# Eight accumulating units multiply in plain fp32 from the loaded weights instead of from a high/low split

## The chip, the cores and the metric

The kernel runs on one core of one Trainium2 chip. The metric is device time in microseconds (us) of one execution; the number shown for a kernel is the median of its runs. Engine names are those of the profile: PE (TensorE), PEld (its weight loads), DVE (VectorE), ACT (ScalarE), POOL (GpSimd), SP (SyncE, here the issuer of most DMAs).

## The reference, cut to what matters

The reference is a three-layer network on 256 tokens of width 2048. The change sits in the first 200 us, in the start of the first layer:

```
mod    = silu(c) @ w_ada + b_ada             # 6 x 2048 values; shift1, scale1 are the first two
h      = rms_norm(x, g) * (1 + scale1) + shift1
proj   = h @ w_in                            # lru_x, lru_gate, q, k, v, g_a, g_b
xc     = causal_depthwise_conv(lru_x)        # then the recurrence, attention, feed-forward, ...
```

Activations are kept transposed (features on the 128 partitions, 256 tokens along the free axis), so a tensor of width 2048 is 16 blocks of 128x256. The first two pieces of `mod` are needed before any block of h exists: block b needs 128 columns of shift1 and of scale1.

## The kernel before, in words

**Units and chunks.** Every matrix product is cut into units of 256 output columns, and a unit into chunks of 512 input rows: a chunk is one DMA of 512 KB, a tile of 128x1024 fp32. Products are made with fp32 split in two parts of a narrower format (fp32r): ACT copies the raw tile to `whi` (L976), DVE subtracts to get `wlo` (L1361), and h is split likewise into Hhi and Hlo. A product is then hi*hi + hi*lo + lo*hi. There are four slots (NSP) for split tiles; ACT and DVE split up to three chunks ahead of PE.

**The first stage, in four quarters.** The eight units `lrux` produce lru_x. They are not done one after the other: quarter q of the input rows (4 blocks of h) is multiplied for all eight units, each unit holding its own PSUM bank through all four quarters (part = open, more, more, close). For each chunk, `products` (L672 to L709) issues 24 matmuls of 128x128 by 128x256: 4 blocks, 2 output halves, 3 products (L690, L691, L692). Only after the last quarter are the banks read out (ACT L1197, DVE L1822). Then come the eight q units, which use `products_wide` (L725, L733).

**Where h comes from.** 16 vector-matrix rows of w_ada per quarter are reduced on DVE: each is a half row block of 128x1024, multiplied with silu(c) (tile CR) and summed in one instruction (L1402, followed by a read of the accumulator). When the sixteenth of a quarter is done, `first_columns` (L1373 to L1382) adds halves and bias and makes A1v, the scale. ACT `norm1` (L987) then computes, per block, Hhi (L991) and a full-precision copy in TG (L995), and DVE subtracts to get Hlo (L1442). The normalised x (XR) comes from DVE L1436, two instructions per quarter. The rms itself needs x to be loaded, eight squares on ACT (L1315), sixteen fp32 products with ones on PE (L910, L911), then DVE L1416, L1421, a root on ACT and a Newton step (L1425 to L1431).

**The stream of loads.** SP issues one DMA after the other from an ordered list, `stream` (L656): first 12 rows for `ada`, then two weight chunks, then 4 more ada, then six times (weight, ada, ada). From there each quarter repeats: two weights, 4 ada, six times (weight, ada, ada); the last quarter has weights only in its second part. Two weights, 4 ada and six triples are 24 loads. In this stage the tiles go round nine raw buffers, so load n must wait until load n-9 is no longer needed, and everything behind it in the list waits too:

```
for el in stream:
    if el.prev >= 0:
        sp.wait_ge(s_freed[done[el.prev][0]], done[el.prev][1])
    sp.dma_start(raw[el.slot][:, 0:el.n], source(el)).then_inc(s_raw[el.slot], 16)
```

A buffer is free when DVE has made wlo from it (`s_lo`) or has reduced it (`s_ada`). Ahead of the list SP issues `vec` (small vectors) and the two halves of c (L649); ACT's queue loads constants (L1304) and x (L1305, 2 MB); POOL's queue loads two small tables. DVE takes its work in the order of the list too (`feed`).

**What else hangs on the stage.** POOL loads four tiles of gate weights (L2046) once all 16 blocks of Hlo exist; PE needs them for the gates (L746), plain fp32 matmuls after the q unit 1 has begun.

Of the kernel before, what the change touches and what calls it, by code (L numbers as in the profile page):

```python
# [89 lines left out]
def _plan():  # L90
# [114 lines left out]
    def weight(un, c):  # L205
        un.chunks.append(len(order))
        order.append(len(stream))
        stream.append(Elem("w", 4 * un.width, (un.src, un.u, un.kc0 + un.corder[c]), ord=len(order) - 1))

    coming = quarter(0)  # L210
    rest = [(b, h) for b in range(32, 96) for h in range(2)]
# [33 lines left out]
    for i, el in enumerate(stream):  # L245
        allowed = [n for k, n in rings if k <= i][-1]
        r = next(r for r in ring if r in allowed)
        ring.remove(r)
        ring.append(r)
        used[r] += 1  # L250
        el.slot, el.landed, el.prev, el.first = r, 16 * used[r], owner.get(r, -1), r not in owner
        owner[r] = i

        key = "ada" if el.kind == "ada" else "split"
        counts[key] += 1
        done.append((key, counts[key]))
# [125 lines left out]
def _build(nc, ctx, d_x, d_mem, d_c, d_vec, d_cst, d_hot, d_relb, d_ada, d_lru, d_w, d_s2, d_out):  # L382
# [110 lines left out]
    s_hi, s_lo, s_mm = sem("hi"), sem("lo"), sem("mm")  # L493

    s_ct, s_cr, s_ada, s_mod = (sem(n) for n in ("ct", "cr", "ada", "mod"))
    s_freed = {"split": s_lo, "ada": s_ada}

    kinds = list(dict.fromkeys(u.kind for u in units))
    s_ev = {k: sem(f"ev_{k}") for k in kinds}
# [7 lines left out]
    s_mup, s_mu, s_sh, s_zc, s_zs, s_totz, s_td, s_cen, s_cenp = (  # L507
        sem(n) for n in ("mup", "mu", "sh", "zc", "zs", "totz", "td", "cen", "cenp"))

    s_xr, s_sl, s_slp, s_hh, s_h, s_hp = (sem(n) for n in ("xr", "sl", "slp", "hh", "h", "hp"))  # L510

    s_sp, s_gt, s_gsb, s_gms, s_pre, s_lg, s_lt, s_ls, s_lm, s_lu, s_la, s_sr, s_scan = (
        sem(n) for n in ("sp", "gt", "gsb", "gms", "pre", "lg", "lt", "ls", "lm", "lu", "la", "sr", "scan"))
# [30 lines left out]
    split_no, mem_no = {}, {}  # L544
    n_split = 0
    for i, el in enumerate(stream):
        if el.kind != "ada":
            n_split += 1
            split_no[i] = n_split
            if el.kind == "mem":  # L550
                mem_no[el.g, el.kt] = n_split
# [93 lines left out]

    def sync(sp):
        sp.dma_start(vec[:, :], d_vec).then_inc(s_vec, 16)
        for h in range(2):
            sp.dma_start(CR[h][:, :], d_c[:, h * CH:(h + 1) * CH]).then_inc(s_c, 16)  # L649
        for el in stream:  # L650
            if el.prev >= 0:
                sp.wait_ge(s_freed[done[el.prev][0]], done[el.prev][1])
            elif el.slot == 5:

                sp.wait_ge(s_lg, 16)
            sp.dma_start(raw[el.slot][:, 0:el.n], source(el)).then_inc(s_raw[el.slot], 16)  # L656
        for b in range(1, NB, 2):
            sp.wait_ge(s_hh, 64 + b + 1)
            sp.dma_start(d_out[:, b - 1:b + 1, :], RES[:, b - 1:b + 1, :]).then_inc(s_out, 16)
        sp.wait_ge(s_out, 8 * 16)  # L660


    def tensor(pe):
# [8 lines left out]
        def products(un, c):  # L672

            ch = un.chunks[c]
            s, w = ch % NSP, un.width
            pe.wait_ge(s_lo, split_no[order[ch]])
            xh, xl, _ = tensors[un.x]
            ps = banks[un.bank]
            start = c == 0 and un.part in ("", "open")
            stop = c == un.nkc - 1 and un.part in ("", "close")  # L680
            for k in range(4):
                kt = 4 * un.corder[c] + k
                if begins[un.x] is un or un.part and un.j == 0:
                    pe.wait_ge(*ready[un.x](kt))
                end = stop and k == 3
                if un.mode == "f":
                    for i in range(2):
                        o, at_ = ps[:, i * 256:(i + 1) * 256], k * w + i * 128
                        h, lo = whi[:, s, at_:at_ + 128], wlo[:, s, at_:at_ + 128]
                        pe.matmul(o, h, xh[:, kt, :], start=start, stop=False, skip_group_check=True)  # L690
                        pe.matmul(o, h, xl[:, kt, :], start=False, stop=False, skip_group_check=True)  # L691
                        ins = pe.matmul(o, lo, xh[:, kt, :], start=False, stop=end and i == 1, skip_group_check=True)  # L692
                        start = False
                elif un.mode == "t":
                    h, lo = whi[:, s, k * w:(k + 1) * w], wlo[:, s, k * w:(k + 1) * w]
                    for t in range(2):
                        o, tk = ps[:, t * 256:(t + 1) * 256], slice(t * 128, (t + 1) * 128)
                        pe.matmul(o, xh[:, kt, tk], h, start=start, stop=False, skip_group_check=True)  # L698
                        pe.matmul(o, xh[:, kt, tk], lo, start=False, stop=False, skip_group_check=True)  # L699
                        ins = pe.matmul(o, xl[:, kt, tk], h, start=False, stop=end and t == 1, skip_group_check=True)  # L700
                        start = False
                else:
                    h, lo = whi[:, s, k * w:(k + 1) * w], wlo[:, s, k * w:(k + 1) * w]
                    o = ps[0:w, 0:256]
                    pe.matmul(o, h, xh[:, kt, :], start=start, stop=False, skip_group_check=True)
                    pe.matmul(o, h, xl[:, kt, :], start=False, stop=False, skip_group_check=True)
                    ins = pe.matmul(o, lo, xh[:, kt, :], start=False, stop=end, skip_group_check=True)
                    start = False
            ins.then_inc(s_mm, 1)  # L709

        def products_wide(un, c):


            ch = un.chunks[c]
            s = ch % NSP
            xh, _, both = tensors[un.x]
            out = [banks[un.bank + i] for i in range(2)]
            pe.wait_ge(s_hi, split_no[order[ch]])
            for k in range(4):
                kt = 4 * un.corder[c] + k  # L720
                if begins[un.x] is un:
                    pe.wait_ge(*ready[un.x](kt))
                for i in range(2):
                    at_ = k * 256 + i * 128
                    pe.matmul(out[i].rearrange("p (a s) -> p a s", a=2), whi[:, s, at_:at_ + 128], both[:, :, kt, :],  # L725
                              start=(c == 0 and k == 0), stop=False, skip_group_check=True)
            pe.wait_ge(s_lo, split_no[order[ch]])
            high = slice(256, 512) if un.x in ("Y0", "Y1") else slice(0, 256)
            for k in range(4):
                kt = 4 * un.corder[c] + k  # L730
                for i in range(2):
                    at_ = k * 256 + i * 128
                    ins = pe.matmul(out[i][:, high], wlo[:, s, at_:at_ + 128], xh[:, kt, :], start=False,  # L733
                                    stop=(c == un.nkc - 1 and k == 3), skip_group_check=True)
            ins.then_inc(s_mm, 1)
# [178 lines left out]
        for st in steps:  # L914
# [22 lines left out]
            elif un.part == "open" and un.bank == 4:  # L937
                clear("S")
            for c in range(un.nkc):
                if un.wide < 0:  # L940
                    products(un, c)
                else:
                    products_wide(un, c)
# [19 lines left out]
    def scalar(act):  # L963
# [21 lines left out]
                                   ACT.Copy).then_inc(s_hi, 1)  # L985

        def norm1(q):  # L987
            act.wait_ge(s_mod, q + 1)
            for b in range(4 * q, 4 * q + 4):
                act.wait_ge(s_xr, b // 2 + 1)  # L990
                act.activation(Hhi[:, b, :], XR[:, b, :], ACT.Identity, scale=A1v[:, b:b + 1],  # L991
                               bias=mod[:, b:b + 1]).then_inc(s_hh, 1)
                if b >= 4:
                    act.wait_ge(s_h, b - 3)
                act.activation(tslot(b), XR[:, b, :], ACT.Identity, scale=A1v[:, b:b + 1],  # L995
                               bias=mod[:, b:b + 1]).then_inc(s_slp, 1)

        def gates(j, n):
            yield from ticks(n)
# [298 lines left out]
        def centre_first(l):  # L1298
# [2 lines left out]
            yield  # L1301
            centred(l, 1)

        act.dma_start(cst[:, 0:C_DUP], d_cst[:, 0:C_DUP]).then_inc(s_cst, 16)  # L1304
        act.dma_start(RES[:, :, :], d_x).then_inc(s_x, 16)  # L1305
        act.wait_ge(s_c, 32)
        for h in range(2):
            act.activation(CT[:, h, :], CR[h][:, :], ACT.Tanh, scale=0.5).then_inc(s_ct, 1)
        act.wait_ge(s_lx, 1)
        act.activation(LPS[:, 3, :], LPS[:, 2, :], ACT.Exp, scale=-1.0).then_inc(s_le, 1)  # L1310
        act.wait_ge(s_x, 16)
        for j in range(8):
            if j >= 2:
# [39 lines left out]
    def vector(dve):  # L1353
# [39 lines left out]
        def feed(upto):  # L1393
            nonlocal pos
            while pos <= upto:
                el, i = stream[pos], pos
                pos += 1
                if el.kind != "ada":
                    low(i, el)
                    continue  # L1400
# [35 lines left out]
                dve.tensor_tensor(XR[:, 2 * j:2 * j + 2, :], RES[:, 2 * j:2 * j + 2, :], over(Rv, 2), ALU.mult).then_inc(s_xr, 1)  # L1436

        def norm1(q):
            for b in range(4 * q, 4 * q + 4):
                dve.wait_ge(s_hh, b + 1)  # L1440
                dve.wait_ge(s_slp, b + 1)
                dve.tensor_tensor(Hlo[:, b, :], tslot(b), v32(Hhi[:, b, :]), ALU.subtract).then_inc(s_h, 1)  # L1442
            if q < 3:
                scaled(q + 1)

        def log1p_exp(e, d, s, q, p, k):

# [449 lines left out]
        for st in steps:  # L1897
# [31 lines left out]
            if un.part in ("open", "more"):  # L1929
                continue  # L1930
            evac(un)
            side.tick()
        side.flush()

# [241 lines left out]
```

## Time and profile before

| what | value |
|---|---|
| median of 3 runs | 2794.49 us (2793.2 to 2797.61) |
| the profiled execution's own time | 2798.37 us |
| its span | 2796.2 us |
| PE busy | 2675.8 us, 96% of the span |
| DVE busy | 1995.4 us, 71% |
| ACT busy | 1449.3 us, 52% |
| DMA, bytes read | 574 MB, 206 GB/s over the span |

Busy time of PE counts from the start of a matmul to a modelled end and overlaps are merged, so a share near 100% need not be PE at its peak: the distance between two starts is the better measure of a matmul. The granted clock of TensorE (PEclk) is 1.00 at 2.4 GHz and 0.50 at 1.2 GHz. Times in the timeline are counted from the start of the span.

### The profile page before, as it was taken

To read this page: it belongs to the slowest core of one execution; us is meant where nothing else is said; L and a number is where in the kernel's file an instruction comes from. 1 tells how busy PE (TensorE), PEld (TensorE's weight loads), DVE (VectorE), ACT (ScalarE), POOL (GpSimd) and SP (SyncE) were. 2 spreads that over 40 slices of the span, in tenths; PEclk is the share of its full clock that TensorE was granted. 3 is DMA by queue.
4 is the path that set the end of the run, shared out by engine and by line. 5 is a ranking of instruction groups with operands and counts; after the bars stand their busy time and mean duration, and the time that the engine had idled before them with its cause. 6 is when DMAs were issued, how large, how long until landed. Compare 5 with 4: busy or idle time off the path is not lost.

```text
span 2796.2 us, 40818 instructions
## 1 busy us (share of the span) xinstructions
PE 2675.8 (96%) x16090; PEld 2360.1 (84%) x16090; DVE 1995.4 (71%) x2806; ACT 1449.3 (52%) x2167; POOL 141.1 (5%) x177
## 2 busy tenths in 40 slices
PE   4789799999999999999999999999999999999996
PEld 4778688888888788888888888888988888889885
DVE  7987888887899866666666676666566766664666
ACT  3355566655545554455545545544554455445543
POOL 0000000000001000000000010100001121000002
PEclk8899899999999999999999999999999999999998
DMA  8964577788889776656566655665546556665452
GB/s 330 375 215 151 173 254 244 264 261 274 289 300 330 260 253 191 194 188 189 183 194 188 189 186 158 190 181 174 155 147 195 182 179 176 182 181 158 143 177 103
DMA packets 162109, 584.10 MB, mean 209 GB/s; under 512 B 19040, under 2 KB 20320, under 8 KB 161792
## 3 DMA queue, kind: packets, MB, share of 16 engines
q1 hardware_dynamic: 157104, 566.86, 62.6%
q0 software_dynamic: 4528, 12.43, 1.6%
q8 instruction: 127, 2.08, 0.3%
q10 hardware_dynamic: 288, 2.23, 0.2%
q14 instruction: 62, 0.51, 0.1%
HBM read 574.05 MB, written 2.15 MB: 206 GB/s over the span
## 4 chain that ended last, share of the span: by engine, by line
PE 83%; DVE 12%; ACT 3%; issue 1%; DMA 0%; ACTq 0%; SPq 0%; DVEq 0%
PE bank L725 47%; PE bank L733 24%; DVE wlo L1361 3%; DVE raw L1402 3%; PE bank L698 2%; PE bank L700 2%; PE bank L699 2%; PE pO L782 1%; PE pS L759 1%; ACT whi L976 1%; PE pT L771 1%; DVE TG L1489 1%; DVE XC L1822 1%; PE pS L812 1%; DVE bank L1808 1%
## 5 line engine op out<-in xcount | busy, mean ns | idle before, releaser
L1361 DVE TENSOR_TENSOR wlo<-raw,whi 128x1024 fp32r<-128x1024 f32 (+1 forms) x880 | 1075.7, 1234 | 447.5 <-ACT whi L976 443.7
L976 ACT ACTIVATE whi<-raw 128x1024 fp32r<-128x1024 f32 (+1 forms) x880 | 911.5, 1048 | 437.1 <-PE bank L733 342.6
L725 PE MATMUL bank<-H,whi 128*128 128x512 f32 x4000 | 1021.1, 397 | 4.5 <-DVE H L1673 3.6
L725 PEld LDWEIGHTS bank<-H,whi 128*128 128x128 f32 x4000 | 724.2, 190 | 146.9 <-issue 6.3
L733 PEld LDWEIGHTS bank<-H,wlo 128*128 128x128 f32 x4000 | 547.7, 191 | 43.5 <-DVE wlo L1361 4.1
L733 PE MATMUL bank<-H,wlo 128*128 128x256 f32 x4000 | 560.2, 283 | 2.1 <-DVE wlo L1361 2.1
L725 PE MATMUL bank<-F,whi 128*128 128x512 f32 x1024 | 256.4, 392 | 0.0
L1402 DVE SCALAR_TENSOR_TENSOR raw<-raw,CR 128x1024 f32<-128x1024 f32 x192 | 231.0, 1220 | 0.0
L725 PEld LDWEIGHTS bank<-F,whi 128*128 128x128 f32 x1024 | 184.1, 189 | 33.0
L1191 ACT ACTIVATE ET<-bank 128x512 f32<-128x512 f32 x116 | 69.2, 596 | 193.9 <-PE bank L733 193.7
L1808 DVE TENSOR_TENSOR bank<-bank,ET 128x512 f32<-128x512 f32 x116 | 81.0, 698 | 96.4 <-ACT ET L1191 96.4
L733 PEld LDWEIGHTS bank<-F,wlo 128*128 128x128 f32 x1024 | 139.7, 190 | 10.0
L733 PE MATMUL bank<-F,wlo 128*128 128x256 f32 x1024 | 142.8, 282 | 0.0
L1191 ACT ACTIVATE EP<-bank 128x512 f32<-128x512 f32 x100 | 59.6, 596 | 146.8 <-PE bank L733 146.7
L1808 DVE TENSOR_TENSOR bank<-bank,EP 128x512 f32<-128x512 f32 x100 | 69.8, 698 | 83.6 <-ACT EP L1191 83.6
L725 PE MATMUL bank<-YY,whi 128*128 128x512 f32 x512 | 128.6, 393 | 0.0
L698 PE MATMUL bank<-whi,H 128*128 128x256 f32 x416 | 121.2, 291 | 4.5 <-DVE wlo L1361 4.5
L699 PE MATMUL bank<-wlo,H 128*128 128x256 f32 x416 | 118.8, 286 | 0.0
L700 PE MATMUL bank<-whi,H 128*128 128x256 f32 x416 | 118.8, 286 | 0.0
L725 PEld LDWEIGHTS bank<-YY,whi 128*128 128x128 f32 x512 | 92.2, 189 | 16.6
L1037 ACT ACTIVATE LP<-LP,SM 128x256 f32<-128x256 f32 (+1 forms) x128 | 57.8, 453 | 71.3 <-DVE SM L1530 46.9
L698 PEld LDWEIGHTS bank<-whi,H 128*128 128x128 f32 x416 | 80.9, 195 | 8.7 <-issue 8.6
(306 smaller groups left out, 2947.8 us busy)
## 6 DMA issues: line engine op xcount, KB each, us to landing
raw<-in_w_in SPq DMA_DIRECT2D x424, 512.0 KB, 4.2
raw<-in_w_ff SPq DMA_DIRECT2D x256, 512.0 KB, 4.3
raw<-in_ada SPq DMA_DIRECT2D x192, 512.0 KB, 5.3
raw<-in_w_out SPq DMA_DIRECT2D x96, 512.0 KB, 4.7
raw<-in_w_lru_out SPq DMA_DIRECT2D x32, 512.0 KB, 4.8
raw<-in_w_attn_out SPq DMA_DIRECT2D x32, 512.0 KB, 5.3
raw<-in_w_kv SPq DMA_DIRECT2D x32, 512.0 KB, 4.5
BT<-gtab POOLq DMA_DIRECT2D x32, 128.0 KB, 4.1
```

What stands on the lines that cost most here:

```text
L698: pe.matmul(o, xh[:, kt, tk], h, start=start, stop=False, skip_group_check=True)
L699: pe.matmul(o, xh[:, kt, tk], lo, start=False, stop=False, skip_group_check=True)
L700: ins = pe.matmul(o, xl[:, kt, tk], h, start=False, stop=end and t == 1, skip_group_check=True)
L725: pe.matmul(out[i].rearrange("p (a s) -> p a s", a=2), whi[:, s, at_:at_ + 128], both[:, :, kt, :], start=(c == 0 and k == 0), stop=False, ...
L733: ins = pe.matmul(out[i][:, high], wlo[:, s, at_:at_ + 128], xh[:, kt, :], start=False, stop=(c == un.nkc - 1 and k == 3), skip_group_chec ...
L759: ins = pe.matmul(pS2[:, i, 0:nk], q, k, start=True, stop=True, skip_group_check=True)
L976: act.activation(whi[:, s, 0:el.n], raw[el.slot][:, 0:el.n], ACT.Copy).then_inc(s_hi, 1)
L1037: ins = act.activation(L[:, i, :], L[:, i, :], ACT.Exp, bias=SM[:, n, 1, i:i + 1], accum_out=SM[:, n, 2, i:i + 1])
L1191: act.activation(spare(un)[:, :, :], half_banks(un, 0 if kind == "y" else 1), ACT.Copy).then_inc(s_e, 1)
L1361: dve.tensor_tensor(wlo[:, s, 0:n], raw[el.slot][:, 0:n], v32(whi[:, s, 0:n]), ALU.subtract).then_inc(s_lo, 1)
L1402: dve.scalar_tensor_tensor(out=raw[el.slot][:, :], in0=raw[el.slot][:, :], scalar=0.5, in1=CR[el.kt][:, :], op0=ALU.mult, op1=ALU.mult, ac ...
L1808: dve.tensor_tensor(ps.rearrange("p (b s) -> p b s", b=2), half_banks(un, 1 if kind == "y" else 0), spare(un)[:, :, :], ALU.add).then_inc( ...
```

## The change

The 32 chunks of the first stage become loads of a kind of their own (`w32`). Nobody splits them: PE multiplies the raw tile with h in fp32, 8 matmuls per chunk, and the raw buffer is free when PE has finished the chunk (`s_mm`). ACT's `norm1` writes h in fp32 in place over XR (semaphore s_hf), and only then copies it to Hhi in one instruction of four blocks; DVE makes Hlo of four blocks in one instruction, a quarter later (the last after the first bank is read out), since it is needed only from the q units on. The second half of c goes to ACT's queue ahead of the constants and x, and an Exp of a small vector is moved ahead of the two Tanh of c.

```diff
@@ stream @@
-        stream.append(Elem("w", 4 * un.width, ...))
+        stream.append(Elem("w32" if un.part else "w", 4 * un.width, ...))
@@ buffers and what frees them @@
+        if el.kind == "w32":
+            done.append(("chunk", el.ord + 1))
+            continue
-    s_freed = {"split": s_lo, "ada": s_ada}
+    s_freed = {"split": s_lo, "ada": s_ada, "chunk": s_mm}
@@ SP @@
-        for h in range(2):
-            sp.dma_start(CR[h][:, :], d_c[:, h * CH:(h + 1) * CH]).then_inc(s_c, 16)
+        sp.dma_start(CR[0][:, :], d_c[:, 0:CH]).then_inc(s_c, 16)
@@ PE @@
+        def products_plain(un):
+            ch = un.chunks[0]
+            el = stream[order[ch]]
+            pe.wait_ge(s_raw[el.slot], el.landed)
+            ps = banks[un.bank]
+            for k in range(4):
+                kt = 4 * un.corder[0] + k
+                if un.j == 0:
+                    pe.wait_ge(s_hf, kt + 1)
+                for i in range(2):
+                    at_ = k * 256 + i * 128
+                    ins = pe.matmul(ps[:, i * 256:(i + 1) * 256], raw[el.slot][:, at_:at_ + 128], XR[:, kt, :],
+                                    start=(un.part == "open" and k == 0 and i == 0),
+                                    stop=(un.part == "close" and k == 3 and i == 1), skip_group_check=True)
+            ins.then_inc(s_mm, 1)
@@ ACT norm1 @@
             for b in range(4 * q, 4 * q + 4):
                 act.wait_ge(s_xr, b // 2 + 1)
-                act.activation(Hhi[:, b, :], XR[:, b, :], ACT.Identity, ...).then_inc(s_hh, 1)
-                if b >= 4:
-                    act.wait_ge(s_h, b - 3)
-                act.activation(tslot(b), XR[:, b, :], ACT.Identity, ...).then_inc(s_slp, 1)
+                act.activation(XR[:, b, :], XR[:, b, :], ACT.Identity, ...).then_inc(s_hf, 1)
+            act.wait_ge(s_hf, 4 * q + 4)
+            act.activation(Hhi[:, 4 * q:4 * q + 4, :], XR[:, 4 * q:4 * q + 4, :], ACT.Copy).then_inc(s_hh, 4)
@@ ACT start @@
+        act.dma_start(CR[1][:, :], d_c[:, CH:2 * CH]).then_inc(s_c, 16)
         act.dma_start(cst[:, 0:C_DUP], d_cst[:, 0:C_DUP]).then_inc(s_cst, 16)
         act.dma_start(RES[:, :, :], d_x).then_inc(s_x, 16)
+        act.wait_ge(s_lx, 1)
+        act.activation(LPS[:, 3, :], LPS[:, 2, :], ACT.Exp, scale=-1.0).then_inc(s_le, 1)
         act.wait_ge(s_c, 32)
@@ DVE @@
+                if el.kind == "w32":
+                    continue
         def norm1(q):
-            for b in range(4 * q, 4 * q + 4):
-                ...
-                dve.tensor_tensor(Hlo[:, b, :], tslot(b), v32(Hhi[:, b, :]), ALU.subtract).then_inc(s_h, 1)
             if q < 3:
                 scaled(q + 1)
+            if q:
+                low1(q - 1)
+        def low1(q):
+            sl = slice(4 * q, 4 * q + 4)
+            dve.wait_ge(s_hh, 4 * q + 4)
+            dve.tensor_tensor(Hlo[:, sl, :], XR[:, sl, :], v32(Hhi[:, sl, :]), ALU.subtract).then_inc(s_h, 4)
@@ DVE, after the read-out of the first bank @@
+            if un.part and un.j == 0:
+                low1(3)
```

## Rows read from the trace of the kernel before

**Rows 1.** Chain of waits, 50 to 75 us: start, length, what
```profile
51.33 1.21 DVE XR L1436 x2
52.53 1.13 DVE wlo L1361
53.67 2.29 DVE raw L1402 x4
```

**Rows 2.** Busy time by windows: window, length, busy per engine, PEclk, DMA share, GB/s
```profile
116.40:150.40 34.00, 25.48 (x192) 25.31 (x193) 30.96 (x51) 12.34 (x17) 0.00 (x0) 0.85 0.96 370
...
62.00:82.00 20.00, 12.00 (x99) 11.68 (x97) 18.67 (x33) 5.53 (x7) 0.00 (x0) 0.88 1.02 410
```

**Rows 3.** Timeline of PE: starts of first and last quarter, idle before in brackets
```profile
48.52 0.55 PE L690 MATMUL bank<-H,whi 128*128 128x256 f32 x1 [24.04 <-DVE H L1442]
...
150.42 0.55 PE L690 MATMUL bank<-H,whi 128*128 128x256 f32 x1 [8.49 <-DVE H L1442]
```

**Rows 4.** Timeline of PE: end of q unit 0
```profile
175.94 2.00 PE L725 MATMUL bank<-H,whi 128*128 128x512 f32 x8
...
178.74 2.00 PE L725 MATMUL bank<-H,whi 128*128 128x512 f32 x8
...
190.06 0.83 PE L919 MATMUL pT<-hot,relb 32*32 32x384 f32 x2
```

**Rows 5.** Timeline of ACT and DVE, the start and the first quarter's columns
```profile
12.40 2.00 ACT L1308 ACTIVATE CT<-CR 128x1024 f32<-128x1024 f32 x2 [9.45 <-DMA CR<-in_c]
...
14.42 1.13 ACT L1315 ACTIVATE TG<-RES 128x512 f32<-128x512 f32 x2
...
28.34 0.42 DVE L1416 TENSOR_SCALAR BT<-pS 128x256 f32<-128x256 f32 x1
...
35.61 1.22 DVE L1402 SCALAR_TENSOR_TENSOR raw<-raw,CR 128x1024 f32<-128x1024 f32 x1
...
45.89 0.09 DVE L1402 DVE_READ_ACCUMULATOR raw<-raw,CR 128x1 f32 x1
...
46.75 0.60 ACT L991 ACTIVATE H<-XR,mod,A1v 128x256 fp32r<-128x256 f32 x1 [13.86 <-DVE A1v L1381]
47.26 0.59 ACT L995 ACTIVATE TG<-XR,mod,A1v 128x256 f32<-128x256 f32 x1
```

**Rows 6.** Timeline of PE: plain fp32 matmuls (two instructions each)
```profile
16.16 1.06 PE L911 MATMUL pS<-TG,cst 128*128 128x256 f32 x2
17.01 1.06 PE L910 MATMUL pS<-TG,cst 128*128 128x256 f32 x2
...
23.88 0.59 PE L911 MATMUL pS<-TG,cst 128*128 128x256 f32 x2
...
193.73 1.02 PE L746 MATMUL pS<-XC,LW 128*128 128x256 f32 x4
194.59 1.03 PE L746 MATMUL pT<-XC,LW 128*128 128x256 f32 x4
```

**Rows 7.** Timeline of PE: fp32r matmuls around the rise of the clock
```profile
52.71 0.41 PE L691 MATMUL bank<-H,whi 128*128 128x256 f32 x1
52.93 0.39 PE L692 MATMUL bank<-H,wlo 128*128 128x256 f32 x1
...
53.28 0.28 PE L691 MATMUL bank<-H,whi 128*128 128x256 f32 x1
53.40 0.28 PE L692 MATMUL bank<-H,wlo 128*128 128x256 f32 x1
```

**Rows 8.** Timeline of SP's DMA queue, 46 to 54 us
```profile
46.01 0.33 SPq L656 DMA_DIRECT2D raw<-in_ada  x1
...
53.69 0.33 SPq L656 DMA_DIRECT2D raw<-in_w_in  x1
```

**Rows 9.** Landing of L656's loads over the run; DMA issues of the start
```profile
DMA to landing us min/median/max: 2.2/4.4/16.8
...
RES<-in_x ACTq DMA_DIRECT2D x1, 2048.0 KB, 10.6
```

More of the change, by code:

```diff
@@ L207, in weight @@
         order.append(len(stream))
-        stream.append(Elem("w", 4 * un.width, (un.src, un.u, un.kc0 + un.corder[c]), ord=len(order) - 1))
+        stream.append(Elem("w32" if un.part else "w", 4 * un.width, (un.src, un.u, un.kc0 + un.corder[c]), ord=len(order) - 1))
     coming = quarter(0)
@@ L508, in _build @@
         sem(n) for n in ("mup", "mu", "sh", "zc", "zs", "totz", "td", "cen", "cenp"))
-    s_xr, s_sl, s_slp, s_hh, s_h, s_hp = (sem(n) for n in ("xr", "sl", "slp", "hh", "h", "hp"))
+    s_xr, s_hf, s_sl, s_hh, s_h, s_hp = (sem(n) for n in ("xr", "hf", "sl", "hh", "h", "hp"))
     s_sp, s_gt, s_gsb, s_gms, s_pre, s_lg, s_lt, s_ls, s_lm, s_lu, s_la, s_sr, s_scan = (
@@ L546, in _build @@
     for i, el in enumerate(stream):
-        if el.kind != "ada":
+        if el.kind in ("w", "mem"):
             n_split += 1
@@ L678, in products @@
             ps = banks[un.bank]
-            start = c == 0 and un.part in ("", "open")
-            stop = c == un.nkc - 1 and un.part in ("", "close")
+            start, stop = c == 0, c == un.nkc - 1
             for k in range(4):
                 kt = 4 * un.corder[c] + k
-                if begins[un.x] is un or un.part and un.j == 0:
+                if begins[un.x] is un:
                     pe.wait_ge(*ready[un.x](kt))
@@ L722, in products_wide @@
                     pe.wait_ge(*ready[un.x](kt))
+                elif un.kind == "q" and un.j == 0 and c == 0:
+                    pe.wait_ge(*ready["H1"](kt))
                 for i in range(2):
@@ L939, in tensor @@
             for c in range(un.nkc):
-                if un.wide < 0:
+                if un.part:
+                    products_plain(un)
+                elif un.wide < 0:
                     products(un, c)
@@ L990, in norm1 @@
                 act.wait_ge(s_xr, b // 2 + 1)
-                act.activation(Hhi[:, b, :], XR[:, b, :], ACT.Identity, scale=A1v[:, b:b + 1],
-                               bias=mod[:, b:b + 1]).then_inc(s_hh, 1)
-                if b >= 4:
-                    act.wait_ge(s_h, b - 3)
-                act.activation(tslot(b), XR[:, b, :], ACT.Identity, scale=A1v[:, b:b + 1],
-                               bias=mod[:, b:b + 1]).then_inc(s_slp, 1)
+                act.activation(XR[:, b, :], XR[:, b, :], ACT.Identity, scale=A1v[:, b:b + 1],
+                               bias=mod[:, b:b + 1]).then_inc(s_hf, 1)
+            act.wait_ge(s_hf, 4 * q + 4)
+            act.activation(Hhi[:, 4 * q:4 * q + 4, :], XR[:, 4 * q:4 * q + 4, :], ACT.Copy).then_inc(s_hh, 4)
         def gates(j, n):
@@ L1308, in scalar @@
             act.activation(CT[:, h, :], CR[h][:, :], ACT.Tanh, scale=0.5).then_inc(s_ct, 1)
-        act.wait_ge(s_lx, 1)
-        act.activation(LPS[:, 3, :], LPS[:, 2, :], ACT.Exp, scale=-1.0).then_inc(s_le, 1)
         act.wait_ge(s_x, 16)
@@ L1438, in norm1 @@
         def norm1(q):
-            for b in range(4 * q, 4 * q + 4):
-                dve.wait_ge(s_hh, b + 1)
-                dve.wait_ge(s_slp, b + 1)
-                dve.tensor_tensor(Hlo[:, b, :], tslot(b), v32(Hhi[:, b, :]), ALU.subtract).then_inc(s_h, 1)
             if q < 3:
                 scaled(q + 1)
+            if q:
[4 more added lines that the diff above has]
+            dve.tensor_tensor(Hlo[:, sl, :], XR[:, sl, :], v32(Hhi[:, sl, :]), ALU.subtract).then_inc(s_h, 4)
         def log1p_exp(e, d, s, q, p, k):
```

## The prediction

> **What bounds the kernel now.** I read the busy shares first (PE 96%), then the chain of waits over the first 200 us, where all of the change lies, then the windows by quarter, then the timelines of PE, DVE, ACT and SP. The chain through a quarter is pure DVE: one subtraction for wlo, two reductions of ada rows, again and again [rows 1]. A window of one quarter is 34.0 us, of which DVE is busy 30.96; the rest it waits for ACT inside norm1. PE works 25.5 us of it and then idles 8.49 us (three times; the last is shown) [rows 2, 3]. But the DMA engines are at a share of 0.96 in the same window [rows 2]: DVE is the bound, and the transfers are right behind it. From the q units on PE is the bound, so what counts is when q unit 0 is finished; before, that is 190.06, where L919 starts [rows 4]. Whatever this point moves, I take the end to move with it.
>
> **The pieces.** A quarter's 24 loads of 512 KB: at 410 GB/s [rows 2] one takes 524 KB / 410 = 1.28 us, all 24 take 30.7 us. A load that finds the engines free lands 4.4 us after its issue (the median over the run) [rows 9]. A reduction is two starts apart, 1.145 us ([rows 1]: four instructions, two reductions, in 2.29).
>
> A plain fp32 matmul of 256 columns: two take 194.59 - 193.73 = 0.86 us, so 0.43 each; at the lower level of the clock 17.01 - 16.16 = 0.85 [rows 6]. A chunk of 8 is 3.44 us at 2.4 GHz. The old chunk of 24 fp32r matmuls, 0.12 apart [rows 7], is 2.88. So PE gets 8 x 0.56 = 4.5 us more per quarter, 27.5 in all, which alone would still fit in 34.
>
> After each idle stretch PE starts at 1.2 GHz: matmuls from 48.52 on are 0.21 to 0.22 apart, and 0.12 apart from 53.28 [rows 3, 7], some 4.7 us, in which half is lost: 2.4 us. Before, that cost nothing, since DVE was the bound. As where the clock rises may vary with the moment of the restart, I allow stretches of 3.6 to 6 us, which gives 1.8 to 3.0. The Trainium skill (TensorE: Matmul & The Clock Gate, What's actually happening) advises to leave this ramp out of a model, as under 1% of a typical span. The trace agrees on the size, yet leaving it out would take 9.6 us off the sum below, and this becomes a rival.
>
> **The start.** c no longer waits behind itself in one queue, and its second half goes ahead of x. Before, ACT had c at 12.40, squared x from 14.42, and the last fp32 product was out by 24.5 (23.88 + 0.59), ten us after the first square [rows 5, 6]. Now c (two halves of 512 KB and 0.2 MB of vec, at some 400 GB/s from about 2.4 on) should be there near 6 us, and its Tanh no longer delays the squares; but x has 512 KB more ahead of it in ACT's queue, so I let it land near 13.5 instead of about 12 (issued near 1.5, 10.6 to landing [rows 9]). The squares' products end near 24.0. DVE: decay and CR are done near 10; the seven ada rows before the rms come at the pace of the transfers and are reduced by 22; then it waits until 24.0. From L1416 (28.34) to the next reduction (35.61) the old trace takes 7.3 us; then 7 reductions, 8.0 us: 39.3. The two wlo that stood here are gone. From the last reduction (45.97) to A1v, one activation and PE is 47.26 - 45.97 + 0.1 = 1.4 us [rows 5]. PE starts at 40.7 instead of 48.52: a gain of 7.8 us. Bounds: 39 if x lands as before, 42.5 if it takes 2 us longer. The Trainium skill (DMA: Bandwidth & Descriptors, Issuing engines are not separate DMA queues) says that a second issuing engine saves issue time only; with c still at 12.4 the seven reductions would end at 24.8, and the sum would be 0.8 us higher. No run here shows the move.
>
> **The quarter, and the step that decides.** DVE falls to 16 x 1.145 = 18.3, plus 0.75 for the columns (45.98 to 46.75 [rows 5]), 1.2 for XR and, by the equal shape of wlo, 1.15 for Hlo [rows 1]: 21.4 us. So it is out of the way. What is late next is the stream of loads. Number a quarter's loads from its first weight: 0 and 1 weights, 2 to 5 ada, 6 weight, 7 and 8 ada, 9 weight, 10 and 11 ada, and so on; the next quarter's PE can start only when its load 29 (24 + 5) is reduced. Load 9 needs the buffer of load 0, load 10 that of load 1. Those were freed by DVE's subtraction, made up to three chunks ahead of PE; even so SP stood still from 46.34 to 53.69 [rows 8]. Now both are freed by PE, which begins only when h is there. With P for PE's start:
> - chunk 1 done at P + 3.44 + 2.4 = 5.8, chunk 2 at P + 9.3; load 10 and all behind it are issued from there
> - load 10 lands at 9.3 + 0.1 + 4.4 = P + 13.8
> - 19 more loads to load 29, 19 x 1.28 = 24.3: P + 38.1
> - reduction 1.15, then 1.4 to PE: P + 40.65.
>
> In between nothing stops the stream longer: load 15 needs chunk 3 (P + 12.7), load 18 chunk 4 (P + 16.2), load 27 chunk 7 (P + 26.5), each before its turn. PE waits 0.3 to 0.7 us a few times for weights, without effect. A quarter thus takes 40.65 us instead of 33.96, three times 6.7 = 20.1 us more. Some 10 us pass between PE's last chunk and its next start, more than the 8.49 of before, so the clock falls again each time.
>
> **The last quarter.** No ada rows; PE is the bound: 8 x 3.44 + 2.4 = 29.9, then q unit 0 with 4 x 2.8 us (178.74 - 175.94 [rows 4]) and 0.2: P + 41.3. Before it was 190.06 - 150.42 = 39.6, with DVE behind on wlo and read-outs: 1.7 us more. Hidden: the read-outs on ACT and DVE (they kept up with one unit in under 4 us with a wlo beside them, and the wlo is gone), ACT's copy to Hhi, the splits for q (DVE is caught up), Hlo's last four blocks at P + 11 (needed at P + 30), POOL's four gate tiles, which now wait for those and are needed at about P + 45 (3.7 us behind L919, as at 193.73 [rows 6]). If that cover failed, PE would wait for 2 MB, some 5 us.
>
> Sum: 40.7 + 3 x 40.65 + 41.3 = 204.0, against 190.06: **+13.9 us**. The profiled execution (2798.37, span 2796.2) would become 2812.3 with a span near 2810; it lies 3.9 above the median of the runs, so the runs become 2794.5 + 13.9 = 2808.4.
>
> **Rivals.**
> - *The ring does not hold* (faster). If the transfers stay ahead in spite of the later release, the quarter falls to the transfers' 30.7 us: 40.7 + 92.1 + 41.3 = 174.1, 16 us faster, 2778.5. For it: SP's stop of 7.4 us in the old trace did not hurt. Against: there nine buffers and three splits of lookahead stood between SP and DVE, and the DMA share was 0.96 all the same. It decides if load 10 is issued before P + 2. Chance 0.09.
> - *The clock does not fall, or the lower level costs nothing*: 2.4 us less in each of four places, +4.3, 2798.8. Against: three gaps of 8.49 us, each followed by matmuls 0.21 apart. 0.06.
> - *Plain fp32 does not raise the clock.* Chunks of 6.84 us; load 27 waits for chunk 7 at P + 47.9, next start at 47.9 + 0.1 + 4.4 + 2 x 1.28 + 2.55 = P + 57.5, end at 40.7 + 172.5 + 54.7 + 11.4 = 279: 2884. Against: L910 and L911 go from 0.85 apart to 0.43 within 4 us of their start. 0.02.
> - The forecast, 0.83. Its own range: the lower clock 1.2 less or 0.6 more in four places, landing 4.4 less or plus 0.5 in three, a load 1.27 to 1.31, the start 39 to 42.5: 2803 to 2813.
>
> Beyond 0.2% (5.6 us) is what a measurement can tell from no change. The forecast is slower by more in nearly all of its range; a shorter lower-clock stretch together with an early start leaks a little to "same". Faster 0.09, same 0.08, slower 0.83. The range takes in the second rival and some scatter of the runs: 2799 to 2814.
>
> **What would show it.** Right: PE's four starts near 41, 81, 122 and 163; SP idle until the end of chunk 2 of each quarter; DVE waiting for `raw` loads; L919 near 204; a wlo count lower by 32. Wrong: starts 31 to 34 us apart (ring does not hold); SP issuing load 10 before PE's first chunk ends; fp32 matmuls not 0.43 apart; or L919 late and the end not, if the q stage has slack that I take it not to have.

## The result, and the profile after

The changed kernel takes 2808.91 us (median of 4 runs, 2807.97 to 2810.51) against 2793.84 (4 runs): ratio 1.0054, 95% interval [1.0038, 1.0070]: slower by half a per cent, clear of the noise. In a second comparison it was 2808.96 against 2795.43: 1.0049 [1.0036, 1.0062]. The forecast was 2808.4, range 2799 to 2814. One of the ten executions of experiment 6 took 15089 us and counts in no ratio.

| | before | changed |
|---|---|---|
| profiled execution, its span | 2798.37, 2796.2 us | 2810.51, 2808.5 us |
| PE's four starts in the first stage | 48.5, 82.5, 116.5, 150.4 | 42.1, 83.9, 125.2, 166.4 |
| end of q unit 0 (L919, now L941) | 190.1 | 207.6 |
| DVE busy, ACT busy | 1995.4, 1449.3 us | 1961.2, 1413.3 us |

Lines have moved: the plain fp32 matmul is L725 of the changed kernel (in the kernel before, L725 was a matmul of the wide products), the ada reductions are L1428, SP's loads L659. The timeline of PE in the changed kernel, every start of a quarter with the idle time before it in brackets, and the end of q unit 0:

```profile
42.10 16.91 PE L725 MATMUL bank<-XR,raw 128*128 128x256 f32 x64 [16.93 <-ACT XR L1016]
...
83.92 16.49 PE L725 MATMUL bank<-XR,raw 128*128 128x256 f32 x64 [9.26 <-ACT XR L1016]
...
166.44 16.19 PE L725 MATMUL bank<-XR,raw 128*128 128x256 f32 x64 [9.25 <-ACT XR L1016]
...
207.55 0.83 PE L941 MATMUL pT<-hot,relb 32*32 32x384 f32 x2
```

These answer to [rows 3, 4]: the first start is 6.4 us earlier, and a quarter takes (166.44 - 42.10) / 3 = 41.4 us where it took 34.0. The windows of one quarter show how (columns: window, length, busy time with count for PE, PEld, DVE, ACT, POOL, then PEclk, DMA share, GB/s):

```profile
42.10:56.50 14.40, 14.40 (x54) 12.20 (x55) 3.27 (x6) 2.39 (x4) 0.00 (x0) 0.80 0.32 112
56.50:81.10 24.60, 17.36 (x76) 13.70 (x74) 15.47 (x26) 0.00 (x0) 0.00 (x0) 0.95 1.02 410
...
125.20:166.40 41.20, 31.20 (x128) 25.48 (x128) 22.51 (x40) 3.12 (x6) 0.00 (x0) 0.87 0.80 306
```

For 14.4 us the DMA engines stand at a share of 0.32, and then they run flat out for 24.6 us at the 410 GB/s of [rows 2]. DVE, once the bound with 30.96 us of 34, is busy 22.5 of 41.2. SP's queue shows what made the gap (start, time, instruction, how many):

```profile
34.88 1.47 SPq L659 DMA_DIRECT2D raw<-in_ada  x2
48.68 0.33 SPq L659 DMA_DIRECT2D raw<-in_w_in  x1
52.13 0.80 SPq L659 DMA_DIRECT2D raw<-in_ada  x2
52.98 0.43 SPq L659 DMA_DIRECT2D raw<-in_w_in  x1
...
90.07 0.33 SPq L659 DMA_DIRECT2D raw<-in_w_in  x1
93.53 0.81 SPq L659 DMA_DIRECT2D raw<-in_ada  x2
...
131.21 0.33 SPq L659 DMA_DIRECT2D raw<-in_w_in  x1
134.66 0.80 SPq L659 DMA_DIRECT2D raw<-in_ada  x2
```

From 36.35 to 52.13 SP issued a single load, at 48.68: that is load 9, released by chunk 1, 6.6 us after PE's start; load 10 goes out at 52.13, 10.0 us after it, with chunk 2. In [rows 8] the stop lasted 7.4 us, here 12.3 and then 3.1 more. The waits over the first 215 us (engine, line, for whom: sum, times, longest) name the new bound, for SP and for DVE:

```profile
SPq L659 <- PE bank L725: 80.3, 16, 14.1
...
DVE raw L1428 <- DMA raw<-in_ada: 58.8, 22, 11.1
```

One trap is in the chain of waits of this quarter:

```profile
67.10 3.73 PE pO L725 x16
70.83 0.02 issue
70.85 0.33 SPq L659
71.18 0.04 issue
71.22 0.43 SPq L659
71.65 0.04 issue
71.69 9.44 DMA raw<-in_ada
```

It steps from the last load onto PE's chunk 7, as if that release were the bound. But the load took 9.4 us from its issue, where one that finds the engines free takes 4.4 [rows 9]: it stood in a queue that had been full since 56.5. What set how far that queue had come is chunk 2, which let it start 19 us before. The sum fits: 52.13 + 4.4 + 19 x 1.28 = 80.85, and DVE starts the last reduction at 81.16.

### The profile page after: what moved, and what is told of

Read it like the earlier page. It is cut to its first block, busy times and chain, and to the rows that moved or that the text cites. A ratio compares the mean times of both kernels' runs of the same rounds, so it can differ in the third digit from the quotient of the medians.

```text
span 2808.5 us, 40182 instructions
## 1 busy us (share of the span) xinstructions
PE 2690.6 (96%) x15834; PEld 2357.2 (84%) x15834; DVE 1961.2 (70%) x2762; ACT 1413.3 (50%) x2123; POOL 141.4 (5%) x177
## 4 chain that ended last, share of the span: by engine, by line
PE 86%; DVE 7%; ACT 3%; DMA 2%; issue 1%; SPq 0%; ACTq 0%; DVEq 0%
PE bank L747 47%; PE bank L755 24%; PE bank L725 2%; PE bank L700 2%; PE bank L701 2%; PE bank L702 2%; DVE wlo L1385 2%; PE pO L804 1%; ACT whi L1000 1%; PE pS L781 1%; DMA raw<-in_ada 1%; DVE TG L1519 1%; DVE raw L1428 1%; DMA raw<-in_w_in 1%; PE pT L793 1%
## 5 line engine op out<-in xcount | busy, mean ns | idle before, releaser
L1385 DVE TENSOR_TENSOR wlo<-raw,whi 128x1024 fp32r<-128x1024 f32 x848 | 1037.0, 1234 | 447.0 <-ACT whi L1000 443.2
L1000 ACT ACTIVATE whi<-raw 128x1024 fp32r<-128x1024 f32 x848 | 878.4, 1048 | 392.4 <-PE bank L755 345.2
L1428 DVE SCALAR_TENSOR_TENSOR raw<-raw,CR 128x1024 f32<-128x1024 f32 x192 | 233.2, 1218 | 60.0 <-DMA raw<-in_ada 58.8
L725 PE MATMUL bank<-XR,raw 128*128 128x256 f32 x256 | 65.9, 425 | 44.7 <-ACT XR L1016 44.7
L725 PEld LDWEIGHTS bank<-XR,raw 128*128 128x128 f32 x256 | 55.2, 217 | 55.4 <-issue 46.2
```

The lines of the kernel that those rows point to most:

```text
L725: ins = pe.matmul(ps[:, i * 256:(i + 1) * 256], raw[el.slot][:, at_:at_ + 128], XR[:, kt, :], start=(un.part == "open" and k == 0 and i == 0),
L1000: act.activation(whi[:, s, 0:el.n], raw[el.slot][:, 0:el.n], ACT.Copy).then_inc(s_hi, 1)
L1385: dve.tensor_tensor(wlo[:, s, 0:n], raw[el.slot][:, 0:n], v32(whi[:, s, 0:n]), ALU.subtract).then_inc(s_lo, 1)
L1428: dve.scalar_tensor_tensor(out=raw[el.slot][:, :], in0=raw[el.slot][:, :], scalar=0.5, in1=CR[el.kt][:, :], op0=ALU.mult, op1=ALU.mult, ac ...
```

## The experiments

"Rest" below is the span less the time at which q unit 0 ends (L919 or its successor).

**1. Late release without fp32.** The kernel before; only who frees the first stage's weight buffers is changed.

```diff
+        if el.kind == "w" and el.ord < 32:
+            done.append(("chunk", el.ord + 1))
+            continue
-    s_freed = {"split": s_lo, "ada": s_ada}
+    s_freed = {"split": s_lo, "ada": s_ada, "chunk": s_mm}
```

> The kernel before with one edit: the raw buffers of the first stage's 32 weight chunks are freed by PE's last matmul of the chunk instead of by DVE's wlo. The split, the fp32r matmuls and c stay. My theory (the later release of the first two weight buffers holds SP's queue, and everything else follows): chunk 2 of a quarter ends 2 x 2.88 + 2.4 = 8.2 us after PE's start; from the issue of the load behind it to PE's next start the changed kernel takes 31.8 us, and here PE starts 1.1 us later than there behind the last reduction (it waits for Hlo): a quarter of 41.1 us instead of 34.0, L919 at 48.5 + 3 x 41.1 + 39.6 = 211, some 21 us later, the time near 2812 to 2815. Rival (the slower quarter comes from the longer work of PE in plain fp32): no fp32 here, quarter stays at 34.0 and the time at 2794. Second rival (DVE bound and nine buffers cover it): within 3 us.

Measured: 2820.08 us, ratio 1.0086 [1.0072, 1.0100]; starts at 48.5, 92.8, 135.1 and 176.6, a quarter of 42.7 us; q unit 0 ends at 215.7. So the release alone, with the old products, costs more than the whole change. Both rivals fall. It came 1.6 us a quarter above my figure, and the time 5 us above the expected band, since here ACT and DVE still split each chunk between its landing and PE, and PE waits for that (longest wait first after the start):

```profile
67.84 0.55 PE L693 MATMUL pS<-H,whi 128*128 128x256 f32 x1 [5.02 <-DVE wlo L1364]
```

That delays the releases behind it as well: in this quarter SP's queue stands still a second time, from 65.5 to 73.3 us, where the changed kernel's longest stop behind load 10 is 2.9 us. So this version is held up by more than the first two buffers.

**2. c alone.** The kernel before with the loads of c and the order of Exp and Tanh of the changed one.

```diff
-        for h in range(2):
-            sp.dma_start(CR[h][:, :], d_c[:, h * CH:(h + 1) * CH]).then_inc(s_c, 16)
+        sp.dma_start(CR[0][:, :], d_c[:, 0:CH]).then_inc(s_c, 16)
+        act.dma_start(CR[1][:, :], d_c[:, CH:2 * CH]).then_inc(s_c, 16)
```

> The kernel before with the loads of c and the order of Exp and Tanh as in the changed kernel, nothing else. The changed kernel began its first product 6.4 us earlier (42.1 against 48.5); two wlo of 1.13 us that went with the split are part of that. So here PE starts near 42.1 + 2.3 + 1.0 (for Hlo) = 45.4 at the latest, 3 to 4 us earlier; the quarters stay 34.0; L919 near 187, time 3 us less, 2790 to 2791. Rival (the queue of transfers stands behind c in any order, so that an earlier c only moves the wait): PE's start at 48 to 48.5 and no change of the time.

Measured: the start is at 44.17, 4.35 us earlier, and q unit 0 ends at 185.8, 4.3 earlier; quarters stay 34. The rival falls for the stage. The time is 2793.54 against 2795.14, ratio 0.9990 [0.9981, 1.0000]: 1.6 us less, which the runs do not clearly tell from nothing, and not the 2790 to 2791 expected.

**3. Half the products.** The changed kernel with fewer matmuls per chunk.

```diff
-            for k in range(4):
+            for k in (0, 2):
```

> The changed kernel, but each chunk of the first stage is multiplied only for blocks 0 and 2 of its four: 4 matmuls instead of 8, half of that product is left out. Loads, buffers and who frees them stay. My theory: chunk 2 ends 3.44 + 2.4 = 5.9 us after PE's start instead of 10.0, 31.8 from there: a quarter of 37.6 us instead of 41.4, although PE now works only about 17 us of it. Last quarter: 8 x 1.72 + 2.4, but then DVE's read-outs bound it (2.9 us a unit and the wlo of q), so some 30 us to L941's chunk work instead of 41. L941 near 42.1 + 112.8 + 36 = 191, time about 2792. Rival (PE's own time sets the quarter): the quarter falls by 8 x 1.72 = 13.8 us to the transfers' 30.7 and L941 comes near 170.

Measured: starts at 41.64, 79.14, 117.22 and 155.17, a quarter of 37.8 us (expected 37.6; by the rival 30.7); q unit 0 ends at 189.8; 2794.02 us, ratio 0.9995 [0.9986, 1.0004]. Before each of the later starts PE is idle for 11 us, longer than in the full version, and still the quarter is longer than the old one:

```profile
79.14 9.75 PE L725 MATMUL bank<-XR,raw 128*128 128x256 f32 x32 [10.98 <-ACT XR L1016]
```

Load 10 goes out 6.3 us after PE's start here (47.94 and 85.47), not 10.0. PE's own time is not what the quarter lacks; of its work only the end of chunk 2 counts.

**4. Buffers of their own.** The changed kernel; the unsplit chunks go to eight tiles in the space of whi and wlo, which this stage no longer uses. The waits that the first splits of q make for PE already guard that space.

```diff
+        if el.kind == "w32":
+            r = NRAW + el.ord % 8
+            ...
+            done.append(("chunk", el.ord + 1))
+            continue
+    raw += [at(f"raw{NRAW + i}", [128, CH], o_w + i * CH * 4) for i in range(8)]
```

> The changed kernel, but the 32 chunks that nobody splits land in eight buffers of their own, the space of whi and wlo, which is idle in this stage; the ada rows keep the nine raw buffers to themselves. My theory: the late release no longer stops SP (a weight's buffer was freed a quarter ago), so PE and the transfers are what is left. PE: 27.5 us a quarter without an idle gap, 29.9 with a restart; transfers 30.7. First quarter started at 42.1; the starts come at 72, 100 to 103, 127 to 133; L941 near 166 to 174 instead of 207.5, 33 to 41 us earlier; time 2767 to 2776, faster than both kernels. Rival (the quarter is set by the ramp of the clock, the fp32 rate or a DMA limit that I have wrong): quarters stay at 38 or more and the time above 2800.

Measured: 2778.94 us, ratio to before 0.9938 [0.9926, 0.9950], faster than both kernels. The starts are at 42.1, 72.7, 100.8 and 131.7, q unit 0 ends at 170.6; both within what was expected. The time is 3 us above the expected band, as the rest is 2606.6 and not 2600.9 as in the changed kernel's profile. Windows and the fourth start of this kernel:

```profile
72.00:100.00 28.00, 28.00 (x131) 24.65 (x130) 19.64 (x38) 0.51 (x1) 0.00 (x0) 1.00 1.03 410
100.00:131.50 31.50, 28.32 (x131) 24.29 (x129) 22.98 (x41) 3.73 (x7) 0.00 (x0) 1.00 1.03 409
131.50:170.50 39.00, 38.84 (x192) 34.20 (x192) 31.69 (x57) 17.68 (x28) 2.15 (x4) 1.00 0.62 220
...
131.66 14.05 PE L731 MATMUL bank<-XR,raw 128*128 128x256 f32 x64 [3.03 <-ACT XR L1022]
```

The transfers never stop, and the gap of 9.25 us is gone, so that the clock stays at 2.4 GHz through the later starts. PE has no gap at all before its second start (72.67), 0.30 us before the third and 3.03 before the fourth.

**5. The same with the edit of 3,** to see what bounds the better version.

> The kernel with eight buffers of their own for the first stage's weights, but each chunk multiplied only for blocks 0 and 2 of its four, half of that product is left out. In the full version the DMA engines are busy at a share of 1.03 from 42 to 131.5 us, and PE waits 3 us before its fourth start. My theory: the transfers bound it, so PE's fourth start stays at 131.7 within 1 us although PE works half as long; the last quarter, with no ada rows, gets shorter, down to DVE's read-outs: L947 near 131.7 + 36 = 167 instead of 170.6, time 2773 to 2777. Rival (PE's plain fp32 bounds it): the fourth start comes at 110 to 118 and the time falls to 2760 or less.

Measured: the fourth start is at 131.45, q unit 0 ends at 166.1, 2772.06 us, ratio 0.9911 [0.9893, 0.9928]. The time is 0.9 us below the expected band. With half of PE's work the third and the fourth start do not move (100.77 and 131.45, against 100.76 and 131.66): there the transfers are the bound. The second start does, from 72.67 to 69.74, so in the first quarter PE's work, begun at the lower clock, was the bound by some 3 us. In the last quarter 13.8 us less work of PE bring only 4.4 us, with PE waiting up to 3.7 us for wlo.

**6. The order of the stream.** The changed kernel; a quarter's last four ada rows stand ahead of its first two weights.

```diff
-            if j == 2:
+            if j == 0:
                 while coming:
                     modulation(*coming.pop(0))
```

> The changed kernel with the stream in another order: the last four ada rows of a quarter stand ahead of its first two weights instead of behind them; buffers, who frees them and the number of loads stay. Then the four loads behind the ninth take buffers of ada rows, which DVE has freed before PE starts, and SP is held only at the buffer of the first weight, with 14 loads to go instead of 20. My theory: the binding release is chunk 3 (P + 13.3 + 0.6), 4.4 and 12 loads of 1.28 and 2.55 on: a quarter of 36 to 36.5 us instead of 41.4; L941 near 42 + 3 x 36.3 + 41.1 = 192, time 2793 to 2796. Rival (the number of nine buffers as such, or the transfer rate, sets the quarter, not whose release comes late): the quarter stays above 40 and the time near 2809.

Measured: 2794.10 us, ratio to before 0.9994 [0.9984, 1.0004]; starts at 42.28, 78.68, 113.56 and 148.44, so quarters of 36.4, 34.9 and 34.9; q unit 0 ends at 190.1. The same loads through the same nine buffers: 15 us come back by the order alone. The mean of 35.4 is 0.9 us a quarter better than the 36.3 of my sum; the gap before a start is 5.2 to 5.6 us here.

**7. The changed kernel with c as before** (the diff of 2, reversed).

> The changed kernel with the loads of c, and Exp behind the Tanh, as before. With c alone PE's first start came 4.35 us earlier (44.17), and the changed kernel's at 42.10. If the two parts add up, the start is here at 42.1 + 4.3 = 46.4, the quarters stay 41.4, L941 near 212, and the time some 4 us above the changed kernel's, 2812 to 2814. Rival (in the changed kernel the transfers are the bound and an earlier c is lost in them): L941 within 1 us of 207.5.

Measured: start at 45.59, quarters of 41.4, q unit 0 ends at 210.7 (3.2 us later than in the first profile of the changed kernel, 4.0 than in the second), 2814.16 us, ratio to before 1.0064 [1.0050, 1.0078], 5.2 above the changed kernel beside it. The earlier c is worth 3.5 us of the start here, 4.35 in experiment 2; it adds to the rest of the change.

**8. The changed kernel again.**

> The changed kernel once more, with more rounds and a second profile. The first profile showed L941 17.5 us later than before, but the span only 12.3 us longer; the missing 5.2 us fall in steps in which one kernel runs at the lower clock after a short wait of PE and the other doesn't. My theory: these steps belong to the single execution. So the starts and L941 (207.5) come within 0.5 us again, while the rest of the span, 2600.9 us behind L941, may come anywhere from 2600 to 2607; the ratio to before lies near 1.005. Rival (the q stage has slack that gives back a fixed part): the rest is again within 1 us of 2600.9.

Measured: 2808.96 us, ratio 1.0049 [1.0036, 1.0062]; starts at 41.84, 83.40, 124.71 and 165.56; q unit 0 ends at 206.7, and it and the fourth start are 0.9 us earlier, where I had allowed 0.5; rest 2601.0. The rest did not scatter, so this alone speaks for the rival, a fixed part given back. The ten profiles together read otherwise. Each one's rest beside its time at the lower clock from 215 us to the end of the span, summed from the granted clock: before 2606.1 (57 us), experiment 4 2606.6 (57), 5 2606.4 (57), 3 2606.9 (57); changed 2600.9 (37), changed again 2601.0 (37), 7 2601.0 (40), 2 2599.7 (40), 1 2601.9 (44), 6 2601.6 (44). Two clusters, 5 us apart: both hold kernels with the old products and with the new, and of two kernels whose q unit 0 ends at 190.1 one is in each. What goes with the cluster is the clock. One of the steps, in windows of the kernel before and then of the changed one, around the same work:

```profile
950.00:970.00 20.00, 15.47 (x65) 12.43 (x64) 16.48 (x26) 10.55 (x16) 0.00 (x0) 0.74 0.71 235
```

```profile
950.00:970.00 20.00, 17.29 (x96) 14.37 (x95) 19.97 (x40) 10.46 (x20) 0.00 (x0) 0.99 0.76 235
970.00:990.00 20.00, 17.94 (x87) 15.26 (x86) 16.88 (x23) 11.16 (x15) 0.00 (x0) 0.84 0.77 253
```

What puts an execution in one cluster stays open; it was not tested apart. It is not the kernel alone: the 36 executions of the kernel before that stand beside the experiments have spans from 2787.6 to 2797.4 us, those with a mean granted clock of 0.984 from 2787.6 to 2791.0 and those at 0.980 from 2795.8 to 2797.4. The nine of the changed kernel lie between 2806.0 and 2809.5, all at 0.984 or 0.985. So the profile of the kernel before (2796.2, at 0.980) is one of its long executions, and against those at 0.984 the changed kernel is behind by about the whole 17.5 us; why it was never seen at 0.980 is not known.

## Why the prediction was right, step by step

- **The step that decides** held: SP's queue stands behind the buffers of the first two weights, which PE frees only after it has begun. Shown by SP's rows, by the release alone (1), by the order (6) and by buffers of their own (4). The chunk behind that wait is the second, as the halved products (3) moved the quarter by 3.6 us and not by 13.8.
- **The quarter**: 40.65 forecast, 41.4 measured. Chunk 2 ended 10.0, 9.6 and 9.4 us after PE's start instead of 9.3: the lower clock lasted longer than the 4.7 us I took, and cost 3.1, 2.7 and 2.5 us instead of 2.4. (For its lower bound the prediction took 1.2 us less in each of the four places, though the stretches that it allows give only 0.6 less; and 3.1 is above the 3.0 that it allows.) From there to the next start it was 31.8 instead of 31.35. Together 2.4 us too little.
- **The start**: 7.8 us gained in the forecast, 6.4 measured. ACT had its x at 14.28, not near 13.5, though c was there by 8.02, and the squares' products ran longer at the lower clock:

```profile
8.02 2.00 ACT L1334 ACTIVATE CT<-CR 128x1024 f32<-128x1024 f32 x2 [1.85 <-DMA CR<-in_c]
...
14.28 1.15 ACT L1339 ACTIVATE TG<-RES 128x512 f32<-128x512 f32 x2 [4.25 <-DMA RES<-in_x]
...
25.21 0.42 DVE L1442 TENSOR_SCALAR BT<-pS 128x256 f32<-128x256 f32 x1 [2.18 <-PE pS L933]
```

  DVE, done with its seven reductions at 23.03, waits 2.18 us for this. With c's second half on ACT's queue c came 4.4 us earlier (12.40 in [rows 5]); the rule from the Trainium skill (DMA: Bandwidth & Descriptors, Issuing engines are not separate DMA queues), by which only issue time is saved, leaves the order among the loads out. The two edits of c were not run apart, so which part is the queue's is open.
- **The last quarter**: 41.3 forecast, 41.1 measured. Plain fp32 matmuls ran at 0.43 us each: 16 instructions, eight of these, from 189.37 to 192.83.
- **The sum**: 13.9 forecast; 17.5 at the end of q unit 0, 12.3 at the end of the span, 15.1 and 13.5 by the medians of the two comparisons. So the closeness of 2808.4 to 2808.9 is partly luck: 3.6 us too little in the first stage, and up to 5 us that I took to be carried to the end ("Whatever this point moves, I take the end to move with it"). That step did not hold between the two profiles: 17.5 us at q unit 0 became 12.3 at the end, along with 37 us at the lower clock behind 215 us in place of 57.
- **The rivals.** "The ring does not hold" put the quarter at the transfers' pace, 30.7, for 2778.5: that is what the kernel of experiment 4 does, where the ring is taken away (2778.9). That the two figures are equal is luck again: its q unit 0 ends at 170.6, not 174.1, and its rest is one of the long ones. "The lower clock costs nothing" is refuted by the 10.0 us that 16 matmuls of 0.43 took. Plain fp32 raised the clock as fp32r had.
- The Trainium skill (TensorE: Matmul & The Clock Gate, What's actually happening) puts the ramp penalty at under 1% of a typical kernel span. The trace agrees: the four ramps are some 10 us of 2808. But a model without them would have given 2798.8, 10 us too low: they are most of the difference between the two kernels.

## What to carry to other kernels

When an operand's consumer changes, so does the moment at which its buffer comes free, and in one ordered queue of loads that moment holds back everything behind it, even what the consumer itself is waiting for. Work removed from the bounding engine (here 8 wlo a quarter on DVE) counts only up to the next bound, so write down for each ring which instruction frees the slot and how many loads stand between that release and the next thing needed. Then a stall can be removed by order or by placement alone: the space that the change made idle held the buffers it lacked.

## What the runs showed of the hardware

- Two loads of 512 KB and one of 2 MB in two queues: c, when both halves stood in SP's queue beside x in ACT's, was there at 12.4 us and x at 11.8; with one half in each queue and ahead of x, c was there at 8.0, and x at 14.3. While both queues had work, from 4 to 10 us of the kernel before, ACT's moved 1.87 MB and SP's 0.43 MB.
- A gap of 9 us on PE brought the lower clock back at every quarter; a gap of 3.0 us in experiment 4 did not (PEclk 1.00 in the window behind it, and its 64 matmul instructions in 14.05 us against 16.2 to 16.9 in the changed kernel).
- The same tail of the kernel took 2600 to 2607 us in ten profiles, in two clusters, along with 37 to 44 or 57 us at the lower clock; the spans of 36 executions of one kernel lay up to 9.8 us apart. A change of 4 us at the start can hide in that, as experiment 2 showed.
